# The order of a head pair's six query tiles in the attention of a diffusion backbone's first mixer

## The reference

```python
def one(qs):
    qnb, qrb = qs
    s = (jnp.einsum("bqhd,bkhd->bhqk", qnb, kn)
         + jnp.einsum("bqhd,bkd->bhqk", qrb, kr)).astype(F32) * scale
    prob = jax.nn.softmax(s, axis=-1).astype(v.dtype)
    return jnp.einsum("bhqk,bkhd->bqhd", prob, v)
...
o = mla_attend(qn, rope2d(qr, rope), jnp.concatenate([kn, knc], axis=1),
               jnp.concatenate([rope2d(kr, rope), krc], axis=1),
               jnp.concatenate([v, vc], axis=1), scale)
...
oc = mla_attend(qnc, qrc, knc, krc, vc, scale)
```

## Time and profile before

| | us |
|---|---|
| median of 3 runs | 3333.2 (3331.41 to 3338.96) |
| profiled execution | 3330.62 |
| its span | 3328.8 |
| TensorE busy, matmuls | 3189.2 (96%) |
| VectorE busy | 1622.4 (49%) |
| ScalarE busy | 963.8 (29%) |
| attention, from its first scores to the output projection | 823.57 to 997.04 |

### The profile page before, as it was taken

How to read it: one execution, slowest core, us unless ns; L and a number is a source line. 1 busy time by engine, 2 the same in 40 slices (tenths; PEclk the granted TensorE clock), 3 DMA queues, 4 the chain that set the end, 5 groups by cost and what they waited for, 6 DMA issues and landing times.

```text
span 3328.8 us, 44389 instructions
## 1 busy us (share of the span) xinstructions
PE 3189.2 (96%) x18259; PEld 2874.2 (86%) x18259; DVE 1622.4 (49%) x2360; ACT 963.8 (29%) x1453; POOL 266.4 (8%) x316
## 2 busy tenths in 40 slices
PE   5999999998999998899999999999999998999999
PEld 5999999986669894488999999999999976678887
DVE  7754536524542736636734355542236547743333
ACT  3211212355441321233212112311212345632222
POOL 1100000200000006620000001000000100000000
PEclk8999999999999999999999999999999999999999
DMA  5533324401004220013523242222224120033332
GB/s 197 173 102 108 120 76 134 133 26 54 1 1 133 63 64 1 1 41 124 158 64 95 76 127 89 89 89 64 63 65 145 57 63 14 2 87 96 95 98 93
DMA packets 381726, 272.91 MB, mean 82 GB/s; under 512 B 17410, under 2 KB 357625, under 8 KB 381433
## 3 DMA queue, kind: packets, MB, share of 16 engines
q1 hardware_dynamic: 356217, 182.50, 18.7%
q0 software_dynamic: 25344, 88.09, 8.0%
HBM read 262.16 MB, written 8.39 MB: 81 GB/s over the span
## 4 chain that ended last, share of the span: by engine, by line
PE 89%; ACT 4%; DVE 3%; issue 2%; POOL 1%; DMA 1%; SPq 0%; ACTq 0%; DVEq 0%
PE ps L458 75%; PE ps L1253 1%; PE ps L1374 1%; PE ps L1148 1%; PE ps L1228 1%; PE ps L1234 1%; PE ps L1244 1%; PE ps L1744 1%; PE ps L1778 1%; PE ps L1761 1%; ACT gpt L1406 1%; PE ps L1745 1%; PE ps L1391 1%; PE ps L1051 1%; PE ps L1751 1%
## 5 line engine op out<-in xcount | busy, mean ns | idle before, releaser
L458 PE MATMUL ps<-u_hi,w_hi 128*128 128x384 f32 (+2 forms) x2992 | 828.4, 346 | 24.2 <-DVE u_lo L600 19.2
L458 PE MATMUL ps<-u_hi,w_lo 128*128 128x384 f32 (+2 forms) x2992 | 822.0, 344 | 0.0
L458 PE MATMUL ps<-u_lo,w_hi 128*128 128x384 f32 (+2 forms) x2992 | 821.4, 344 | 0.0
L448 DVE TENSOR_TENSOR w_lo<-ring,w_hi 128x1024 fp32r<-128x1024 f32 (+3 forms) x357 | 415.6, 1165 | 796.6 <-ACT w_hi L433 602.3
L458 PEld LDWEIGHTS ps<-u_hi,w_hi 128*128 128x128 f32 x2992 | 540.9, 189 | 54.5 <-issue 28.0
L458 PEld LDWEIGHTS ps<-u_lo,w_hi 128*128 128x128 f32 x2992 | 541.7, 189 | 22.7 <-issue 1.7
L458 PEld LDWEIGHTS ps<-u_hi,w_lo 128*128 128x128 f32 x2992 | 541.8, 189 | 20.9
L433 ACT CAST w_hi<-ring 128x1024 fp32r<-128x1024 f32 (+3 forms) x229 | 221.6, 969 | 991.8 <-PE ps L458 945.5
L458 PE MATMUL ps<-hid_hi,w_hi 128*128 128x384 f32 (+1 forms) x1232 | 339.3, 344 | 0.0
L458 PE MATMUL ps<-hid_lo,w_hi 128*128 128x384 f32 (+1 forms) x1232 | 338.4, 344 | 0.0
L458 PE MATMUL ps<-hid_hi,w_lo 128*128 128x384 f32 (+1 forms) x1232 | 338.1, 344 | 0.0
(11 more groups left out here) (267 smaller groups left out, 3340.5 us busy)
## 6 DMA issues: line engine op xcount, KB each, us to landing
ring<-in_w_ff_in SPq DMA_DIRECT2D x176, 512.0 KB, 3.7
m_in<-in_w_mod POOLq DMA_DIRECT2D x128, 512.0 KB, 3.7
ring<-in_w_ff_out SPq DMA_DIRECT2D x64, 512.0 KB, 3.5
ring<-in_w_in_e SPq DMA_DIRECT2D x26, 512.0 KB, 3.7
ring<-in_w_ff_out SPq DMA_DIRECT2D x32, 384.0 KB, 3.0
m_first<-in_w_mod POOLq DMA_DIRECT2D x16, 512.0 KB, 12.9
ring<-in_w_out_e SPq DMA_DIRECT2D x16, 512.0 KB, 3.8
ring<-in_w_in_o SPq DMA_DIRECT2D x12, 512.0 KB, 3.7
```

The source lines that it names most:

```text
L448: dve.tensor_tensor(w_lo[:, b:b + WIDE[n]], ring[:, s:s + WIDE[n]], w_hi[:, b:b + WIDE[n]], ALU.subtract).then_inc(w_split_lo, 1)
L458: mm = pe.matmul(ps_at(p, c0, c1) if halved else pair(p)[:, c0:c1], w, x[:, c0:c1], start=start and i == 0, stop=stop and i == 2)
```

## The change

One expression in the building of `units`: within each head pair the tiles come in the order 0, 4, 1, 2, 5, 3 in place of 0, 1, 2, 3, 4, 5. Both heads of a tile still follow each other. The three engines' loops are untouched and follow the list.

```diff
         units = []
         for qt_hh in range(MH * NT):
-            hp, qt, e = qt_hh // (2 * NT), qt_hh % (2 * NT) // 2, qt_hh % 2
+            hp, qt, e = qt_hh // (2 * NT), (0, 4, 1, 2, 5, 3)[qt_hh % (2 * NT) // 2], qt_hh % 2
             hh = 2 * hp + e
```

## The result

The changed kernel takes 3343.49 us (median of 15 executions, 3340.87 to 3348.12), the kernel before 3332.59 beside it (15, 3329.13 to 3338.96): ratio 1.003, 95% interval 1.0023 to 1.0037. A second comparison on another chip gave 3341.36 against 3334.93, ratio 1.0023 (1.0014 to 1.0032). It is slower, by 0.2 to 0.3 per cent. The profiled execution has a span of 3339.1 against 3328.8.

The account below looks back on a forecast made before the run. TensorE, with 89% of the chain, was taken as the bound; its attention waits, 7 x 2.12 + 4.76 + 0.74 = 20.34 us against 14.06, gave +6.3 and 3339.5 us. Range 3334.5 to 3344.0.

Parts of the forecast that it names:

- dearer seam: Rival: first odd token step keeps its 0.81 wait after every context pair; +3.7 us, 3343.2; chance 0.10.
- Interior: Groups of six units inside the attention: TensorE waits 2.12 us per context pair, 4.24 per head pair against 3.24.
- The wait that goes (0.81): First odd token step behind a context pair: the old order's 0.81 us wait before the transposes disappears.
- the next one late (0.29): Following even token step: rope products newly wait 0.29 us for the exp of the odd unit before.
- Start: First context pair, behind units 0 and 1: rope products wait 0.86 us longer, next step -0.12; fill +0.74.
- Drain: Attention's end, now on token units: TensorE waits of 2.14, 1.31 and 1.31 us, 4.76 against 2.72.
- Sum of the waits: All TensorE waits in the attention behind the first fill: new 20.34 us, old 14.06, so +6.3.
- the granted clock of 1.00 in the drain: Sign to look for at the attention's end: TensorE keeps its full granted clock, 1.00.
- wait of kind (3): After a token output product, out copy and next probT copy must pass; 0.86 us, twice in each head pair.
- the gain: Rival: short units let ScalarE and VectorE catch up, waits inside the groups vanish; 14.8 us less, 3324.7; chance 0.05.
- The margin of 0.07: First odd token step behind a context pair: work 2.91 us against a chain of 2.84, so no wait.
- The clock: Rival: TensorE's clock falls to 1.2 GHz in the longer drain; +1.7 us, 3341.2; chance 0.17.

Follow-up runs that it names:

- only last head pair new: Kernel before with the new tile order in its last head pair only, head pairs 0 to 2 old: attention 176.91 us, +3.44; ratio 1.0013.

## Why the prediction came out as it did

The time lies inside the range (3343.5 in 3334.5 to 3344.0), four us above the forecast, and the kernel is slower where I had given "same" two points more than "slower". That it lies inside is in part luck: the range's upper end stood where it did for a dearer seam, which did not come, and the fallen clock used up that room to within 0.5.

- Interior. Forecast 2.12 us of waits per group of six and head pairs 43.3 apart; measured 21.66 per group, 43.3. The wait that goes (0.81) is gone, the next one late (0.29) is there with 0.31.
- Start. Forecast +0.74. After, rope products behind scores (0.52 of work) leave 0.97 of wait, and the transposes of unit 1 behind the next scores (0.45) another 0.99:

```profile
828.96 0.70 PE L1228 MATMUL ps<-kn,qn 128*128 128x256 f32 x2 [0.77 <-ACT prob L1264]
830.45 0.48 PE L1234 MATMUL ps<-kr,qr 64*128 64x256 f32 x1 [0.80 <-ACT prob L1264]
...
831.79 0.60 PE L1228 MATMUL ps<-kn,qn 128*128 128x256 f32 x2
833.23 0.85 PE L1244 MATMUL ps<-cst,prob 128*128 128x128 f32 x6 [0.84 <-ACT probT L1278]
```

Before, the same subtraction (with 1.38 and 1.31) gives 0.12 and 1.08, so that the start costs +0.76:

```profile
828.87 1.56 PE L1228 MATMUL ps<-kn,qn 128*128 128x512 f32 x4 [0.77 <-ACT prob L1264]
830.37 0.69 PE L1234 MATMUL ps<-kr,qr 64*128 64x512 f32 x1
...
832.57 1.46 PE L1228 MATMUL ps<-kn,qn 128*128 128x512 f32 x4
834.96 0.85 PE L1244 MATMUL ps<-cst,prob 128*128 128x128 f32 x6 [0.94 <-ACT probT L1278]
```

- Drain. Forecast, from the last scores to the last output product, 4.15, 1.16 + 1.31 and 2.06 + 1.31, together 9.99; the "only last head pair new" kernel has 4.24, 2.45 and 3.24, together 9.93. In the changed kernel with the fallen clock the same three are 4.24, 3.52 and 4.82.
- Sum of the waits. Forecast +6.3, measured +6.5 with the clock held at 1.00.
- Of the signs that I had named, two did not come: the granted clock of 1.00 in the drain, and by it the first product of the output projection near 1003.3, which stands at 1006.28. The period, the wait of kind (3) twice in each head pair, the wait of the rope products and the missing wait at the first odd token step are there.
- The dearer seam and the gain: neither came. The margin of 0.07 at the first odd token step held in each group.
- The clock. This is the term that was missized. I had made it a rival with 0.17 and 1.7 us, in the drain only. It fell in the drain in both profiled executions of the changed kernel, cost 2.66 and 1.50 there, and fell at the start too in one of them, for 0.81. Three things were wrong. The price was taken as the 1.7 us of clock lost in one row; the first fall in the drain was twice as large (3.4 us of clock missing) and cost 2.66, since transposes, copy and output product follow each other there and two of the three rounds went at the lower clock. The second, with 1.7 missing, cost 1.50, near the price. The start was not examined, although its two waits of 0.97 and 0.99 lie side by side. And it was treated as a case by itself, yes or no, where it belongs into the sum with its frequency; the sum had it at nothing. With half of the starts and three fifths of the drains falling, at 0.81 and at the mean of 2.66 and 1.50, some +1.7 on average is an estimate from these few executions, 8.2 with the waits; the two comparisons, 10.0 and 7.7 by their ratios, lie on both sides of it.
- What I read against it, that the old drain kept 1.00 with 2.25 of 4 us of work, was one execution, and the "only last head pair new" kernel shows 1.34 of 4 keeping 1.00 as well. Such a row does not exclude a fall in the next execution.
- The Trainium skill, page "TensorE: Matmul & The Clock Gate", section "Part 4: PE-mode transpose", has the rule by which the prediction let the fall come: that transposes in transpose mode don't count as activity in the way other matmuls do. It came in three of five drains on token units that were not filled; the direction agrees, it came in none of six drains on context units although they have transposes too, and nothing here tells transposes from other matmuls.
- About 1 us of the first profiled pair lies behind the attention, where both kernels are the same. From the output projection's start to the end of the span the kernels here take 2331.8 to 2335.8; before stands at the lower end, and so does one of the reordered kernels ("only last head pair new"). I take it for scatter and not for the change.

## What to carry to other kernels

In a software pipeline over units of two sizes, short units cost at the borders of their run: at its entry, because the long copies of the units before have less TensorE work to hide under, and at its exit, because the long softmax of the next unit has. That is what the waits here show. Mixing them finely makes more borders; put them into few runs, and the last run at the end, where the pipeline drains with short steps. And before reordering the units look for what an in-order engine does between two links of the chain: one exchange of two copies on ScalarE was worth more here (7.75 us) than any order (5.22).

## What the runs showed of the hardware

The granted clock of TensorE can drop to 1.2 GHz behind stretches that are about half empty (1.88 of 4 us busy in the drain, 2.44 of 4 at the start), without a single wait above 2.12 us, and the same instructions with the same waits keep 2.4 GHz in another execution (the start of the changed kernel in one of its two profiles). A fall costs less than the clock that is missing: 2.66 us of 3.4 and 1.50 of 1.7 in the drain, where transposes, copy and output product follow each other, and 0.81 of 1.7 at the start.
